# A feed-forward down product in passes of 512 columns in place of two of 256

## The reference

```python
def conv_ffn(x, ffn_w_in, ffn_conv_w, ffn_conv_b, ffn_w_out):
    u, gt = jnp.split(x @ ffn_w_in, 2, axis=-1)
    a = dwconv(gt, ffn_conv_w) + ffn_conv_b
    return (jax.nn.silu(a) * u) @ ffn_w_out
```

## Time and profile before

| | |
|---|---|
| time, median of 3 runs | 1636.41 us (1634.76 to 1636.46) |
| span of the profiled execution | 1634.2 us |
| median less span | 2.2 us |
| TensorE busy (matmul) | 1620.2 us, 99% |
| VectorE busy | 1155.2 us, 71% |
| ScalarE busy | 868.8 us, 53% |
| matmuls of the down products, L663 | 1584 of 13642 |
| mean granted TensorE clock | 0.999 of full speed |

### The profile page before, as it was taken

One profiled execution on the slowest core, in us unless ns is written; L12 is line 12 of the kernel. 1 busy time (PEld: TensorE's weight loads), 2 busy tenths in 40 slices (PEclk: granted clock), 3 DMA queues, 4 the chain that ended last, 5 costly groups with the idle time before them and its releaser, 6 DMA issues.

```text
span 1634.2 us, 32191 instructions
## 1 busy us (share of the span) xinstructions
PE 1620.2 (99%) x13642; PEld 1584.0 (97%) x13642; DVE 1155.2 (71%) x1730; ACT 868.8 (53%) x1305; POOL 40.5 (2%) x59
## 2 busy tenths in 40 slices
PE   9999999999999999999999999999999999999998
PEld 9999999999999999999999999999999999999998
DVE  6588778658666767977974866568576545877777
ACT  5456544646444454555355644455755555464554
POOL 3030000000000000000000000000000000000000
PEclk9999999999999999999999999999999999999999
DMA  9984456535656564445564465655454453556562
GB/s 313 305 213 155 149 197 248 194 130 187 209 173 206 168 238 168 161 149 188 201 234 160 151 227 178 207 173 186 163 173 168 155 180 132 192 168 207 173 204 102
DMA packets 83071, 305.85 MB, mean 187 GB/s; under 512 B 10704, under 2 KB 10832, under 8 KB 80752
## 3 DMA queue, kind: packets, MB, share of 16 engines
q1 hardware_dynamic: 77280, 279.44, 50.1%
q0 software_dynamic: 5648, 24.35, 5.0%
HBM read 300.52 MB, written 6.29 MB: 188 GB/s over the span
## 4 chain that ended last, share of the span: by engine, by line
PE 90%; DVE 7%; issue 1%; ACT 1%; DMA 0%; SPq 0%; DVEq 0%; ACTq 0%
PE general L621 56%; PE general L625 14%; PE scores L663 5%; PE attention_out L663 3%; PE probs_transposed L663 3%; DVE weights_lo L1622 2%; PE attention_out L815 2%; PE scores L748 1%; PE probs_transposed L767 1%; PE scores L839 1%; ACT weights_hi L1166 1%; DVE x_tok L1696 1%; DVE x_tok L1693 1%; DVE xT_lo_part L1632 1%; PE attention_out L859 1%
## 5 line engine op out<-in xcount | busy, mean ns | idle before, releaser
L1622 DVE TENSOR_TENSOR weights_lo<-raw_weights,weights_hi 128x1024 fp32r<-128x1024 f32 x525 | 633.4, 1222 | 372.0 <-ACT weights_hi L1166 369.4
L1166 ACT ACTIVATE weights_hi<-raw_weights 128x1024 fp32r<-128x1024 f32 x525 | 553.2, 1058 | 390.6 <-PE general L621 219.0
L621 PE MATMUL general<-xT_hi_part,weights_hi 128*128 128x256 f32 x2432 | 683.4, 281 | 2.3 <-DVE weights_lo L1622 2.0
L621 PE MATMUL general<-xT_lo_part,weights_hi 128*128 128x256 f32 x2432 | 674.8, 277 | 0.0
L621 PE MATMUL general<-xT_hi_part,weights_lo 128*128 128x256 f32 x2432 | 674.7, 277 | 0.0
L621 PEld LDWEIGHTS general<-xT_hi_part,weights_hi 128*128 128x128 f32 x2432 | 457.4, 188 | 10.5 <-issue 8.8
L621 PEld LDWEIGHTS general<-xT_lo_part,weights_hi 128*128 128x128 f32 x2432 | 457.2, 188 | 1.4 <-issue 1.0
L621 PEld LDWEIGHTS general<-xT_hi_part,weights_lo 128*128 128x128 f32 x2432 | 458.0, 188 | 0.0
L1965 DVE SCALAR_TENSOR_TENSOR exp_ring<-general,param_cols,exp_ring 128x255 f32<-128x255 f32 (+1 forms) x176 | 76.8, 478 | 46.2 <-ACT exp_ring L1362 44.7
L1362 ACT ACTIVATE exp_ring<-general,param_cols 128x256 f32<-128x256 f32 x88 | 44.9, 561 | 69.6 <-PE general L621 69.6
L625 PE MATMUL general<-weights_hi,xT_hi_part 128*128 128x256 f32 x272 | 76.6, 281 | 0.0
(11 more groups left out here) (328 smaller groups left out, 2947.4 us busy)
## 6 DMA issues: line engine op xcount, KB each, us to landing
raw_weights<-in_stream SPq DMA_DIRECT2D x525, 512.0 KB, 4.2
attention_area<-in_ln_rows POOLq DMA_DIRECT2D x9, 1024.0 KB, 5.2
bias_scratch<-in_rpb POOLq DMA_DIRECT2D x32, 96.0 KB, 10.5
attention_area<-bias_scratch POOLq DMA_DIRECT2D x2, 1536.0 KB, 8.9
memT_hi<-memT_scratch POOLq DMA_DIRECT2D x2, 1024.0 KB, 5.0
memT_lo<-memT_scratch POOLq DMA_DIRECT2D x2, 1024.0 KB, 8.8
attention_area<-in_mem SPq DMA_DIRECT2D x2, 512.0 KB, 6.0
z_tok<-in_x SPq DMA_DIRECT2D x1, 1024.0 KB, 10.5
```

Of the source, the lines that this page charges most:

```text
L621: ins = nc.tensor.matmul(ps[b][0:m, half * T:half * T + T], w[wk][:, half * m:half * m + m], x[xk_], start=first, stop=last, skip_group_ch ...
L1166: nc.scalar.activation(hi_half(h), raw_half(h), ACT.Copy).then_inc(*hi_done.more())
L1622: nc.vector.tensor_tensor(lo_half(h), raw_half(h), hi_half(h).bitcast(F32), ALU.subtract).then_inc(*lo_done.more())
```

## The change

For each block (kc, t, c) the loop over the two column ranges q is gone. Each of the three matmuls has all 512 columns of the block as its moving operand and writes the whole bank. The start flag is set on the very first matmul into a bank, as before, the stop flag on the last. The waits, the semaphores raised and the order of blocks stay.

```diff
-                    for q in range(2):
-                        for n, (xk_, wk) in enumerate(((0, 0), (0, 1), (1, 0))):
-                            at = c * 512 + q * TILE_N
-                            ins = nc.tensor.matmul(down[2 * t + c][:, q * TILE_N:q * TILE_N + TILE_N],
-                                                   act[xk_][:, kc, t * P:t * P + P], w[wk][:, at:at + TILE_N],
-                                                   start=(i + kc + q + n == 0), stop=(last and kc + q == 2 and n == 2),
-                                                   skip_group_check=True)
+                    at = slice(c * 512, c * 512 + 512)
+                    for n, (xk_, wk) in enumerate(((0, 0), (0, 1), (1, 0))):
+                        ins = nc.tensor.matmul(down[2 * t + c][:, :], act[xk_][:, kc, t * P:t * P + P], w[wk][:, at],
+                                               start=(i + kc + n == 0), stop=(last and kc == 1 and n == 2),
+                                               skip_group_check=True)
```

## The result

The changed kernel takes 1639.37 us (median of 20 runs, 1638.05 to 1640.49), the kernel before 1636.49 us (20 runs, 1634.76 to 1637.67). The ratio is 1.0017, with a 95% interval of 1.0010 to 1.0023: slower by about 3 us, where 14 us less were forecast. The profiled execution of the changed kernel is the quickest of its 20; its span is 1636.3 us, 2.1 us more than that of before, where the medians differ by 2.9.

What follows compares the result with a forecast made beforehand. TensorE was taken to bound the kernel; 29 down products at 0.47 us less (13.7 us) plus 0.4 us gave 14.1 us saved, a span of 1620.1 us and, with 2.2 us added, 1622.3 us; range 1618 to 1633.5 us.

Steps and rivals of the forecast that it cites:

- What bounds the kernel: Whole kernel: TensorE, busy 1620.2 of 1634.2 us; the changed line L663 is 11% of the chain.
- The price of a wide pass: Down products: a 512-column fp32r matmul costs 216 ns, as L815; each product 5.65 to 5.18 us.
- a floor of 109 to 118 ns per instruction: Narrow matmuls: pace set by loading 128 stationary columns, which 256 fp32r columns fail to hide.
- The bound of 235.5 ns: Down products: upper price of a 512-column matmul, twice the old 117.7 ns, no gain.
- rival 3: Down products: columns carry the cost, 235.5 ns, no change, 1636.4 us; chance 0.07 together with the skill's rule.
- The Trainium skill's rule: Down products: a pair of matmuls loses only 2.5 ns, about 2 us in all, 1634.7 us; counted within rival 3's 0.07.
- Rival 1, the neighbours: Gate and value matmuls behind down products stay slow, 11.30 instead of 10.90 us per 96; 10.8 us given back, 1633.1 us; chance 0.16.
- main case: Whole kernel: 216 ns per wide matmul, 14.1 us saved, 1622.3 us, own range 1618.5 to 1625 us; chance 0.62.
- The rival on the slow side: Down products: wide fp32r passes take 430 ns, a product 10.3 us, about 1772 us in all; chance 0.04.
- The tails: Block ends: VectorE sets the pace, so three last products gain nothing in full; the third block's final 24 matmuls gain 0.4 us.

Runs made afterwards that it cites:

- the nudged kernel before: Kernel before plus one extra 128-column fp32r matmul between each of 27 down products and the 96 gate and value matmuls behind it: 1644.44 us, ratio 1.0049.
- the ladder: Kernel before plus extra matmul groups behind its end, results unused; one 256-column form took 5.65 us per 48 behind f32 matmuls, 5.44 behind quick activations-moving matmuls.

## Why the prediction was wrong

**What bounds the kernel.** Right: the down products are on the chain, and nothing else came up behind them.

**The price of a wide pass.** This is the step that failed. "I take 216 ns, since L815 is the nearest row" gave 13.7 of the 14.1 us. The pass measured 233 ns. L815 streams as long, but it is an f32 form with 256 columns, and what was priced there is one of the two records of an f32 matmul; fp32r columns cost 0.43 to 0.46 ns each, more than the 0.417 of one per cycle at 2.4 GHz, and the f32 record shows hardly any such excess. The reading behind it, "a floor of 109 to 118 ns per instruction, set by loading 128 stationary columns, which 256 fp32r columns fail to hide", was wrong for 256 columns: with 64 stationary columns 117 of 118 ns were left. The transposes did not show that floor either. They are f32 forms (the code moves `z_tok`, an f32 tensor), and their 109 ns for 128 columns lie on one line with the 215 for 256 and the 430 for 512, about 0.84 ns per column; that this is near the narrow 113 ns is chance. The bound of 235.5 ns, called "no gain", was nearly what came: rival 3, at 0.07, is the mechanism; products gave 27 x 0.06 = 1.6 us. The Trainium skill's rule (TensorE: Matmul & The Clock Gate, Back-to-back issue gap) would have saved 2.5 ns a pair, 60 ns a product; the trace agrees on the saving (5.65 to 5.59) but not on the distances, 233 ns where it has 215.8. The agreement may be luck: it holds against narrow passes at the slow pace, while against two at the quick pace (226.7 ns) the wide one costs 6 ns more.

**Rival 1, the neighbours.** Right as a mechanism and given 0.16: 14 of 27 groups were slow, 5.5 us on the chain (the last counts half) of the 10.8 set for all. It had been weighed against the wrong main case. "Against it that the 96 now find the quick pace after every down product" mistook one repeated sequence for an attraction: the nudged kernel before shows how little it takes to leave it.

**Both together** were not put down as one case: no gain from the passes and half of rival 1. That is 1634.2 - 1.6 + 5.5 = 1638.1 us of span, 1640.3 with the 2.2 us beyond it, and gives a slower kernel; the median is 1639.37. The rival on the slow side, wide passes at half rate (430 ns), was far off.

**The tails.** Right: VectorE paces the end of the first block (1.39 us per bank) and its last split holds up the last product of the third. Wrong in the sum: "12 x 216 = 2.59 us: 0.4 us gained". The 2.99 us it was set against also hold the late start of the first matmul and the end of the last, which 12 x 216 leaves out, and the narrow matmuls between ran near the quick pace in before (21 steps from 1623.33 to 1625.72 us, 114 ns each), where nothing was left to gain. The wide ones took 3.05 us.

**Open.** What in the array or its reads makes two paces, and why a sequence of forms settles in one of them, no run here tells; nor why a wide pass with weights moving takes 229 ns behind the kernel and 233 in it.

## What to carry to other kernels

A row of another data type does not tell what the columns of the new form cost, and its records need not be one per matmul. Where no row has the form, take the distance at the old width times the columns as the likeliest price, not as the far bound: here that is 235.5 ns, and 233 came. Halving the number of instructions pays only as far as the old form is shown to wait for something other than its own columns, and the way to show that is to shorten the suspected thing (64 stationary columns here, which moved 256 columns by 1 ns). In a kernel that TensorE bounds to 99%, differences of 4% between stretches with equal instructions are worth a look before the change: they can be larger than the change and move when it is made. A trace is one execution: before a difference of 2 us between two traces is explained, look how much of it lies in stretches that the change does not touch.

## What the runs showed of the hardware

Narrow fp32r matmuls of one and the same form run at 113.3 or 117.8 ns, with the clock granted in full and, in the ladder, with the other engines idle. In the kernel before, down products keep one pace and gate and value products the other through all three blocks; 0.11 us of extra work or a single wide block changes that, and the same code took either pace (21.79 or 22.62 us for 192 matmuls) in two executions. The changes with no work in them (another order of pairs, an operand twice) left the time where it was (ratios 1.0004 and 0.9997), while one matmul of 0.11 us in 27 places cost 8.2 us, 3.0 for itself and 5.3 for the pace. And an fp32r pass of 512 columns costs 228 to 233 ns, 229 and 228 of them without accumulation and with 64 stationary columns; an f32 matmul of 256 columns costs 432, in two records of 216.
